# The first loads of a trunk layer split over two queues, and another warm-up of TensorE

## The chip, the cores and the metric

The kernel runs on one core of one Trainium2 chip. The metric is the device time of one execution in microseconds (us), as the median of several runs. Engines are called PE or TensorE (matrix products), DVE or VectorE, ACT or ScalarE, POOL or GpSimd, and SP or SyncE, which only issues transfers here. SPq and ACTq are the queues of transfers that SyncE and ScalarE issue.

## The reference

One layer of a streaming encoder over x of 1024 rows by 1024 features, all in f32:

```python
h = rms_norm(x, mix_norm_g)
proj = h @ w_in                      # columns: u (512), v (512), q (512), k (128), value (128)
y_a = gelu(u) * (W_s layer_norm(gelu(v)) + b)      # W_s: 128 x 128 per group, lower block triangle
y_b = attention over a window of 128 rows, 8 heads, 2 of keys, with sinks and a bias by offset
x = x + concat(rms_norm(y_a), rms_norm(y_b)) @ w_out
h = rms_norm(x, ffn_norm_g)
x = x + (silu(h @ w_gate) * (h @ w_up)) @ w_down   # 2816 features between
return rms_norm(x, final_norm_g)
```

What matters here is the first product only: the v columns of `h @ w_in`. The kernel takes the norm apart. The norm's weight per feature (`mix_norm_g`) is multiplied into the rows of `w_in`, and the root of the mean square per row of x is applied to the result afterwards, so that the products can start on the raw x.

## The kernel before, in words

Each f32 operand is split into a high part, rounded to the type fp32r, and a low part, the rest. A product is then three products in fp32r: high by high, high by low, low by high. ScalarE makes the high part with an activation of the kind Copy (for weights with the norm's weight as scale), VectorE makes the low part by subtracting the high part from the scaled raw data.

The work is written out by hand: every engine has its list of instructions in program order, and semaphores tie them together. No planner is involved. The stage that the change touches is the very first one.

- x arrives transposed, as `xT`, in two halves of 512 rows (h = 0, 1), each in 8 blocks of 128 features (k = 0 to 7). A block is 128 x 512 f32, 256 KB. It goes to `hT_raw[h][:, k]`.
- The v columns of `w_in` arrive in 8 blocks of 128 features by 512 columns, also 256 KB each, in `wv_raw` (line 340). The norm's weights `mix_gT`, 4 KB, go to `mix_g`, a part of the tile `small` (line 339).
- SyncE issues all of this (lines 336 to 340): x block 0, the norm's weights, v block 0, x block 1, v block 1, and so on. The semaphore `block_in[k]` counts 16 for each landed block of k. Behind them it issues the transfers for the attention's bias (`rel_rep`), eight small setup transfers, x's second half and x by rows (`xs`).
- ScalarE (lines 1049 to 1051) takes for each k first x's block (`xT_block`, line 1014), which waits for both blocks of k, then the weights' block (`wv_block`, line 1019). VectorE (lines 1442 to 1444) takes for each k `xT_lo` (line 1391) and then `wv_block` (line 1395).
- PE first runs a warm-up of 20 transposes of the identity (lines 709 to 711), which waits for the identity that POOL makes with a memset and a select (lines 551 to 554). Then come the twelve products of block 0: four of high x by high weights (line 716), four of low x by high weights (line 719), four of high x by low weights (line 722). Blocks 1 to 7 follow through `gate_block`, twelve products each (lines 687 to 689), and block 5 is followed by five transposes of setup data (lines 728 and 730) that need the identity.
- `ones` is a tile of 128 x 128 ones, set by POOL at line 574 and used in the middle of the stage for a sum over rows (line 739). The semaphore `zero_ready` counts this memset and two others.
- The semaphore `block_in[k]` is used again later, for x's second half and for weights of the output projection, with counts that go on from the ones before.

Of the kernel before, what the change touches and what calls it, by code (L numbers as in the profile page):

```python
# [24 lines left out]
def hybrid_trunk_layer(nc, x, xT, mix_gT, w_in, sgu_ln_g, sgu_ln_b, sgu_w, sgu_b, sinks, rel_bias,  # L25
# [3 lines left out]
    P = 128  # L29
    ROWS, D = x.shape  # L30
    T = ROWS // P
    K = D // P
    DA = sgu_ln_g.shape[0]
# [15 lines left out]
    HT = T // 2  # L49
# [4 lines left out]
    def at(name, kb, shape, dtype=F32):  # L54
        n = 4
        for s in shape[1:]:
            n *= s
        offset = BASE + int(kb * 1024)
        assert offset + n <= nc.sbuf_usable_end, name
        return nc.alloc_sbuf_tensor_at(name, shape, dtype, offset=offset)  # L60
# [3 lines left out]
    hT_hi = [at(f"hT_hi{h}", 32 * h, [P, K, C], F32R) for h in range(2)]  # L64
    hT_lo = [at(f"hT_lo{h}", 32 * h + 16, [P, K, C], F32R) for h in range(2)]
    hT_raw = [at(f"hT_raw{h}", 32 * h + 16, [P, K, C]) for h in range(2)]
    wv_hi, wv_lo = at("wv_hi", 64, [P, K, C], F32R), at("wv_lo", 80, [P, K, C], F32R)
# [6 lines left out]
    wv_raw = [at(f"wv_raw{j}", 144 + 4 * j, [P, 2, C]) for j in range(4)]  # L74
# [7 lines left out]
    ident = at("ident", 200.5, [P, P])  # L82
# [3 lines left out]
    vecs, ones = at("vecs", 206, [NV, P]), at("ones", 206.5, [P, P])  # L86
# [64 lines left out]
    def cols(n):  # L151
        c0[0] += n
        assert c0[0] <= 256
        return small[:, c0[0] - n:c0[0]]
# [9 lines left out]
    minus_half, mix_g = cols(T), cols(K)  # L164
# [14 lines left out]
    w_in_k = w_in.rearrange("(k p) n -> p k n", p=P)  # L179
# [60 lines left out]
        return NP * i + IDX[p, m] + 1  # L240


    WARM = 20

    ROOT_BANK, MIX_BANK = (2, 7), (3, 6)

# [2 lines left out]
    with ExitStack() as ctx:  # L249
        ps = ctx.enter_context(nc.psum_tensor("ps", [P, 8, C], F32))  # L250

        def sem(name):
            return ctx.enter_context(nc.semaphore(name))

        ident_set, ident_ready, consts_ready, zero_ready = (sem(n) for n in ("ident_set", "ident_ready", "consts_ready", "zero_ready"))
        mixg_in, rel_in, setup_in, ffng_in, fin_in = (
            sem(n) for n in ("mixg_in", "rel_in", "setup_in", "ffng_in", "fin_in"))
        bias_out, bias_in, rel_built = sem("bias_out"), sem("bias_in"), sem("rel_built")
        setup_T, gains_ready, wT_copied, wT_ready, rowsum_done, Bc_ready, sinks_ready = (
            sem(n) for n in ("setup_T", "gains_ready", "wT_copied", "wT_ready", "rowsum_done", "Bc_ready", "sinks_ready"))  # L260
# [2 lines left out]
        x_sq, x_mse, x_rstd, rstd_T, roots_ready, hT_hi_ready, hT_ready = (  # L263
            sem(n) for n in ("x_sq", "x_mse", "x_rstd", "rstd_T", "roots_ready", "hT_hi_ready", "hT_ready"))

        block_in = [sem(f"block_in{k}") for k in range(K)]
        wv_hi_ready, wv_split = sem("wv_hi_ready"), sem("wv_split")
        va_done, v_ready, v_bn, v_stats, v_mse, v_rstd, vn_ready = (
            sem(n) for n in ("va_done", "v_ready", "v_bn", "v_stats", "v_mse", "v_rstd", "vn_ready"))
# [38 lines left out]
        def _(sp):  # L308
# [5 lines left out]
            def xT_load(h, k):  # L314
                if h:
                    sp.wait_ge(hT_hi_ready, k + 1)
                sp.dma_start(hT_raw[h][:, k, :], xT[h, k]).then_inc(block_in[k], 16)
# [16 lines left out]
                        sp.dma_start(raw[n % 2][:].rearrange("p (k n) -> p k n", k=K), w_in_k[:, :, col:col + P]).then_inc(raw_in[n % 2], 16)  # L334

            for k in range(K):
                xT_load(0, k)
                if k == 0:
                    sp.dma_start(mix_g, mix_gT).then_inc(mixg_in, 16)
                sp.dma_start(wv_raw[k // 2][:, k % 2, :], w_in_k[:, k, DA:2 * DA]).then_inc(block_in[k], 16)  # L340
            sp.dma_start(rel_rep[:].rearrange("p b h -> p (b h)"),
                         rel_bias.rearrange("b h -> (b h)").partition_broadcast(CH)).then_inc(rel_in, 16)
            sp.dma_start(vecs[0:HA, :], group_norm_g[0:DA].rearrange("(k p) -> k p", p=P)).then_inc(setup_in, 16)
# [197 lines left out]
            n = 0  # L541
# [6 lines left out]

        @block.gpsimd
        def _(pool):  # L550
            nc.gpsimd.memset(ident[:], 0.0).then_inc(ident_set, 1)
            nc.gpsimd.memset(minus_half, -0.5).then_inc(consts_ready, 1)
            pool.wait_ge(ident_set, 1)
# [17 lines left out]
                nc.gpsimd.tensor_tensor(rstd_v[:, r:r + 1], ms_v[:, r:r + 1], minus_half[:, 0:1], ALU.pow).then_inc(v_rstd, 1)  # L571

            pool.wait_ge(consts_ready, 1)
            nc.gpsimd.memset(ones[:], 1.0).then_inc(zero_ready, 1)
            nc.gpsimd.memset(kT[:, 0:CH], 0.0).then_inc(zero_ready, 1)
            nc.gpsimd.memset(vT[:, 0:CH], 0.0).then_inc(zero_ready, 1)
            pool.wait_ge(rel_in, 16)
# [105 lines left out]
        def _(pe):  # L683
            mm = nc.tensor.matmul
# [6 lines left out]
            def gate_block(h, k):  # L691
                pe.wait_ge(hT_ready, K * h + k + 1)
                if h == 0:
                    pe.wait_ge(wv_split, k + 1)
                for t in range(HT):
                    rows = slice(t * P, (t + 1) * P)
                    last = split_mm(ps[:, HT * h + t, :], (hT_hi[h][:, k, rows], hT_lo[h][:, k, rows]), (wv_hi[:, k], wv_lo[:, k]), k == 0, k == K - 1)
                    if k == K - 1:
                        last.then_inc(va_done, 1)
# [6 lines left out]
                    last = nc.tensor.transpose(ps[:, ROOT_BANK[h], t * P:(t + 1) * P], rstd_x[:, r:r + 1].to_broadcast([P, P]), ident[:])  # L706
                last.then_inc(rstd_T, 1)

            pe.wait_ge(ident_ready, 1)
            for n in range(WARM):  # L710
                nc.tensor.transpose(ps[:, 0, 0:P], ident[:], ident[:])

            pe.wait_ge(hT_hi_ready, 1)
            pe.wait_ge(wv_hi_ready, 1)
            for t in range(HT):
                mm(ps[:, t, :], hT_hi[0][:, 0, t * P:(t + 1) * P], wv_hi[:, 0], start=True, stop=False)  # L716
            pe.wait_ge(hT_ready, 1)
            for t in range(HT):
                mm(ps[:, t, :], hT_lo[0][:, 0, t * P:(t + 1) * P], wv_hi[:, 0], start=False, stop=False)
            pe.wait_ge(wv_split, 1)  # L720
            for t in range(HT):
                mm(ps[:, t, :], hT_hi[0][:, 0, t * P:(t + 1) * P], wv_lo[:, 0], start=False, stop=False)
            for k in range(1, K):
                gate_block(0, k)
                if k == 5:
                    pe.wait_ge(setup_in, 112)
                    for h in range(HA):
                        last = nc.tensor.transpose(ps[:, 5, h * P:(h + 1) * P], sgu_raw[:, h, :], ident[:])
                    last.then_inc(setup_T, 1)
                    nc.tensor.transpose(ps[:, 4, 0:NV], vecs[:], ident[0:NV, 0:NV]).then_inc(setup_T, 1)  # L730
# [274 lines left out]
        def _(act_e):  # L1005
# [4 lines left out]
                actv(xs[r % 4][:], xs[r % 4][:], ACT.Square, accum_out=ssq_x[:, r:r + 1]).then_inc(x_sq, 1)  # L1010

            def xT_block(h, k):
                act_e.wait_ge(block_in[k], 48 if h else 32)
                actv(hT_hi[h][:, k, :], hT_raw[h][:, k, :], ACT.Copy).then_inc(hT_hi_ready, 1)

            def wv_block(k):
                if k == 0:
                    act_e.wait_ge(mixg_in, 16)
                actv(wv_hi[:, k, :], wv_raw[k // 2][:, k % 2, :], ACT.Copy, scale=mix_g[:, k:k + 1]).then_inc(wv_hi_ready, 1)

            def gated_rows(r):
# [8 lines left out]
            def item(c):  # L1030
# [9 lines left out]
                else:  # L1040
# [5 lines left out]
                        last = actv(w_hi[SLOT[c]][:, k, :], raw[n % 2][:, k * P:(k + 1) * P], ACT.Copy, scale=mix_g[:, k:k + 1])  # L1046
                    last.then_inc(item_hi, 1)

            for k in range(K):
                xT_block(0, k)  # L1050
                wv_block(k)
            for r in range(HT):
                xT_block(1, 2 * r)
                square(r)
                xT_block(1, 2 * r + 1)
# [90 lines left out]
                actv(ps[:, 6, :], ps[:, 6, :], ACT.Square, accum_out=ssqB[:, r:r + 1]).then_inc(yb_squared, 1)  # L1146

            def woB_piece(t):
                act_e.wait_ge(block_in[t], 80)
                if t == 0:  # L1150
                    act_e.wait_ge(unit_done, NU)
                actv(woB_hi[:, t, :], woB_raw[t][:], ACT.Copy, scale=grp_g[:, HA + t:HA + t + 1]).then_inc(woB_hi_ready, 1)
# [53 lines left out]
            for _half in probabilities(1):  # L1206
                pass
            woB_piece(0)
            yb_square(0)
            woB_piece(1)  # L1210
            woB_piece(2)

            for r in range(T):
# [171 lines left out]
        def _(dve):  # L1385
# [3 lines left out]
            def xT_lo(h, k):  # L1389
                dve.wait_ge(hT_hi_ready, K * h + k + 1)  # L1390
                tt(hT_lo[h][:, k, :], hT_raw[h][:, k, :], hT_hi[h][:, k, :].bitcast(F32), ALU.subtract).then_inc(hT_ready, 1)

            def wv_block(k):
                dve.wait_ge(wv_hi_ready, k + 1)
                stt(wv_lo[:, k, :], wv_raw[k // 2][:, k % 2, :], mix_g[:, k:k + 1], wv_hi[:, k, :].bitcast(F32), ALU.mult, ALU.subtract).then_inc(wv_split, 1)
# [44 lines left out]
                last.then_inc(sinks_ready, 1)  # L1440

            for k in range(K):
                xT_lo(0, k)
                wv_block(k)
            xT_lo(1, 0)
            setup_copies()
            for k in range(1, K):
# [414 lines left out]
```

## Time and profile before

| | us |
|---|---|
| median of 3 runs | 939.16 |
| lowest and highest | 938.81, 939.39 |
| the profiled execution | 939.3 |
| its span, first to last instruction | 937.5 |
| PE busy | 927.8 |
| DVE busy | 550.2 |
| ACT busy | 409.1 |
| POOL busy | 318.1 |

The span is what the profiler sees between the first and the last instruction; the profiled execution's own time is a little longer, since it holds what lies around the span. Busy time counts an engine's instructions, the warm-up's too. For an idle time the profile names what ended it, the releaser. A matmul's listed duration includes its way through the array, so that the products of a row overlap: their pace is read from the starts.

### The profile page before, as it was taken

What the parts mean: (1) busy time and instruction counts of PE and PEld (TensorE: products, weight loads), DVE (VectorE), ACT (ScalarE), POOL (GpSimd) and SP (SyncE); (2) the same over time, 40 slices, a digit from 0 to 9 for tenths busy, and PEclk for the clock granted to TensorE, in tenths of its full rate; (3) what the DMA queues carried; (4) which work ended last, traced back from release to release, by engine and by line L of the source; (5) the groups of instructions that cost most, each with busy time, mean ns of one, the idle gap of its engine ahead of it and who ended that gap; (6) DMA issues with size and microseconds to landing.
All of it is one profiled execution on the core that took longest, in us unless ns stands there. A gap on an engine that the chain in (4) does not pass through costs nothing.

```text
span 937.5 us, 12052 instructions
## 1 busy us (share of the span) xinstructions
PE 927.8 (99%) x4327; PEld 763.8 (81%) x4327; DVE 550.2 (59%) x798; ACT 409.1 (44%) x896; POOL 318.1 (34%) x330
## 2 busy tenths in 40 slices
PE   9999999999999999999999999999999999999997
PEld 7888888878788788888888888888888888888885
DVE  5754653476676995574645546546455766545653
ACT  6843560456554733333333333333245354444351
POOL 1410000000005396585674955747554100000022
PEclk9999999999999999999999999999999999999999
DMA  9621231411214425537346274373648996665643
GB/s 328 225 78 64 71 80 64 90 46 66 93 48 154 124 77 193 162 107 237 112 157 220 65 233 142 116 224 100 193 159 279 334 389 194 193 199 186 199 134 136
DMA packets 131999, 147.03 MB, mean 157 GB/s; under 512 B 16280, under 2 KB 92644, under 8 KB 131940
## 3 DMA queue, kind: packets, MB, share of 16 engines
q1 hardware_dynamic: 131412, 145.87, 47.9%
q8 instruction: 35, 0.57, 0.2%
q10 hardware_dynamic: 528, 0.39, 0.1%
q14 instruction: 24, 0.20, 0.1%
HBM read 105.73 MB, written 40.50 MB: 156 GB/s over the span
## 4 chain that ended last, share of the span: by engine, by line
PE 97%; DVE 1%; issue 0%; DMA 0%; ACT 0%; SPq 0%; DVEq 0%; POOLq 0%; POOL 0%; ACTq 0%
PE ps L687 31%; PE ps L689 31%; PE ps L688 31%; PE ps L889 1%; PE ps L816 1%; PE ps L762 1%; PE ps L835 1%; PE ps L826 1%; DVE woB_lo L1578 0%; PE ps L842 0%; PE ps L770 0%; DMA wv_raw<-in_w_in 0%; PE ps L780 0%; PE ps L716 0%; DVE small L1556 0%
## 5 line engine op out<-in xcount | busy, mean ns | idle before, releaser
L1654 DVE TENSOR_TENSOR P_lo<-P_raw,P_hi 128x512 fp32r<-128x512 f32 x132 | 120.6, 929 | 79.8 <-ACT P_hi L1199 78.6
L687 PE MATMUL ps<-T_hi,P_hi 128*128 128x512 f32 x352 | 137.0, 389 | 0.4 <-issue 0.4
L689 PE MATMUL ps<-T_hi,P_lo 128*128 128x512 f32 x352 | 136.9, 389 | 0.0
L688 PE MATMUL ps<-T_lo,P_hi 128*128 128x512 f32 x352 | 136.9, 389 | 0.0
L687 PE MATMUL ps<-rb_hi,ra_hi 128*128 128x512 f32 x308 | 119.8, 389 | 0.0
L688 PE MATMUL ps<-rb_lo,ra_hi 128*128 128x512 f32 x308 | 119.8, 389 | 0.0
L689 PE MATMUL ps<-rb_hi,ra_lo 128*128 128x512 f32 x308 | 119.8, 389 | 0.0
L635 POOL TENSOR_TENSOR wd<-wd 128x256 f32<-128x256 f32 x88 | 79.7, 905 | 96.3 <-DMA wd<-in_w_down 91.1
L1297 ACT ACTIVATE ra_hi<-ra 128x512 fp32r<-128x512 f32 x77 | 48.6, 631 | 99.2 <-DMA rb<-w_down_T 62.0
L558 POOL TENSOR_SCALAR small<-small 128x1 f32<-128x1 f32 (+2 forms) x11 | 2.2, 197 | 225.0 <-ACT ps L1146 131.2
L687 PEld LDWEIGHTS ps<-T_hi,P_hi 128*128 128x128 f32 x352 | 66.1, 188 | 14.5 <-issue 0.8
L1199 ACT ACTIVATE P_hi<-P_raw 128x512 fp32r<-128x512 f32 x132 | 76.6, 620 | 2.1 <-POOL P_raw L606 2.1
L688 PEld LDWEIGHTS ps<-T_lo,P_hi 128*128 128x128 f32 x352 | 66.1, 188 | 13.7
L689 PEld LDWEIGHTS ps<-T_hi,P_lo 128*128 128x128 f32 x352 | 66.1, 188 | 13.6
L1732 DVE TENSOR_TENSOR ra_lo<-ra,ra_hi 128x512 fp32r<-128x512 f32 x77 | 55.4, 720 | 36.7 <-ACT ra_hi L1297 36.3
L687 PE MATMUL ps<-B,P_hi 128*128 128x512 f32 x176 | 68.8, 391 | 0.4 <-DVE P_lo L1654 0.4
L558 POOL TENSOR_SCALAR late<-late 128x1 f32<-128x1 f32 x12 | 5.8, 484 | 184.8 <-ACT junk L1365 178.9
L688 PE MATMUL ps<-B,P_hi 128*128 128x512 f32 x176 | 68.5, 389 | 0.0
L689 PE MATMUL ps<-B,P_lo 128*128 128x512 f32 x176 | 68.5, 389 | 0.0
L689 PEld LDWEIGHTS ps<-rb_hi,ra_lo 128*128 128x128 f32 x308 | 57.8, 188 | 12.1
L687 PEld LDWEIGHTS ps<-rb_hi,ra_hi 128*128 128x128 f32 x308 | 57.8, 188 | 12.0
L688 PEld LDWEIGHTS ps<-rb_lo,ra_hi 128*128 128x128 f32 x308 | 57.8, 188 | 11.9
(200 smaller groups left out, 1944.8 us busy)
## 6 DMA issues: line engine op xcount, KB each, us to landing
wd<-in_w_down SPq DMA_DIRECT2D x44, 256.0 KB, 3.4
w_down_T<-wd SPq DMA_DIRECT2D x22, 512.0 KB, 5.1
ra<-act_S SPq DMA_DIRECT2D x44, 256.0 KB, 2.7
rb<-w_down_T SPq DMA_DIRECT2D x44, 256.0 KB, 3.0
act_S<-Q SPq DMA_DIRECT2D x33, 256.0 KB, 3.7
ra<-act_A SPq DMA_DIRECT2D x33, 256.0 KB, 4.7
rb<-in_w_down SPq DMA_DIRECT2D x33, 256.0 KB, 5.6
P_raw<-in_w_gate SPq DMA_DIRECT2D x22, 256.0 KB, 3.9
```

Of the source, the lines that this page charges most:

```text
L635: nc.gpsimd.tensor_tensor(wd[:, d, :], wd[:, x, :], wd[:, y, :], ALU.subtract).then_inc(wd_summed, 1)
L687: mm(dst, lhs[0], rhs[0], start=start, stop=False, skip_group_check=onto)
L688: mm(dst, lhs[0], rhs[1], start=False, stop=False, skip_group_check=onto)
L689: return mm(dst, lhs[1], rhs[0], start=False, stop=stop, skip_group_check=onto)
L762: last = mm(ps[:, MIX_BANK[m % 2], t * P:(t + 1) * P], vn[:, HT * half + t, h * P:(h + 1) * P], sgu_wT[:, h, :], start=True, stop=True)
L816: last = mm(ps[:, 3 + g, (2 * ci + tp) * P:(2 * ci + tp + 1) * P], q, kT[rows, c * CH:c * CH + WIN], start=True, stop=True)
L826: last = nc.tensor.transpose(ps[:, 5, (2 * g + tp) * P:(2 * g + tp + 1) * P], S[:, g, ci, tp, :], ident[:])
L835: last = mm(ps[g * DH:(g + 1) * DH, 6, ci * G * CH:(ci + 1) * G * CH], V2[:, 2 * r + ci, g, :], pT[:, ci, g * G * CH:(g + 1) * G * CH], st ...
L1199: actv(w_h[p, m][:], src[:], ACT.Copy).then_inc(w_hi_ready, 1)
L1297: actv(ra_hi[n][:], ra[n][:], ACT.Copy).then_inc(step_hi, 1)
L1654: tt(w_l[p, m][:], src[:], w_h[p, m][:].bitcast(F32), ALU.subtract).then_inc(w_split, 1)
L1732: tt(ra_lo[n][:], ra[n][:], ra_hi[n][:].bitcast(F32), ALU.subtract)
```

## The change

- v's blocks 0, 1 and 2 and the norm's weights are issued by ScalarE, ahead of its first activation: block 0, the norm's weights, block 1, block 2. A new semaphore `wv0_in`, in the place of `mixg_in`, counts v's block 0 and the norm's weights. SyncE issues x's blocks 0 to 2 one after the other, and from k = 3 on v's block ahead of x's.
- ScalarE and VectorE take the weights' block ahead of x's for each k. In block 0, PE takes high x by low weights second and low x by high weights last.
- The warm-up is 10 products of `ones` with 64 columns of `ones`, into another bank (7), and waits for the memset of `ones`, which POOL now does first of all. The wait for the identity moves to block 5.
- Because `block_in[0]` now counts only x's block, the later waits on these semaphores go by the list `LOADED`.

```diff
-    WARM = 20
+    WARM, WARM_N = 10, 64
...
+        LOADED = [16 if k == 0 else 32 for k in range(K)]
...
             for k in range(K):
+                if k >= 3:
+                    sp.dma_start(wv_raw[k // 2][:, k % 2, :], w_in_k[:, k, DA:2 * DA]).then_inc(block_in[k], 16)
                 xT_load(0, k)
-                if k == 0:
-                    sp.dma_start(mix_g, mix_gT).then_inc(mixg_in, 16)
-                sp.dma_start(wv_raw[k // 2][:, k % 2, :], w_in_k[:, k, DA:2 * DA]).then_inc(block_in[k], 16)
...
         def _(pool):
+            nc.gpsimd.memset(ones[:], 1.0).then_inc(zero_ready, 1)
             nc.gpsimd.memset(ident[:], 0.0).then_inc(ident_set, 1)
...
             pool.wait_ge(consts_ready, 1)
-            nc.gpsimd.memset(ones[:], 1.0).then_inc(zero_ready, 1)
...
-            pe.wait_ge(ident_ready, 1)
+            pe.wait_ge(zero_ready, 1)
             for n in range(WARM):
-                nc.tensor.transpose(ps[:, 0, 0:P], ident[:], ident[:])
+                mm(ps[:, 7, 0:WARM_N], ones[:], ones[:, 0:WARM_N], start=True, stop=True)
...
                 mm(ps[:, t, :], hT_hi[0][:, 0, t * P:(t + 1) * P], wv_hi[:, 0], start=True, stop=False)
+            pe.wait_ge(wv_split, 1)
+            for t in range(HT):
+                mm(ps[:, t, :], hT_hi[0][:, 0, t * P:(t + 1) * P], wv_lo[:, 0], start=False, stop=False)
             pe.wait_ge(hT_ready, 1)
             for t in range(HT):
                 mm(ps[:, t, :], hT_lo[0][:, 0, t * P:(t + 1) * P], wv_hi[:, 0], start=False, stop=False)
-            pe.wait_ge(wv_split, 1)
-            for t in range(HT):
-                mm(ps[:, t, :], hT_hi[0][:, 0, t * P:(t + 1) * P], wv_lo[:, 0], start=False, stop=False)
             for k in range(1, K):
                 gate_block(0, k)
                 if k == 5:
+                    pe.wait_ge(ident_ready, 1)
...
             def xT_block(h, k):
-                act_e.wait_ge(block_in[k], 48 if h else 32)
+                act_e.wait_ge(block_in[k], LOADED[k] + 16 * h)
...
                 if k == 0:
-                    act_e.wait_ge(mixg_in, 16)
+                    act_e.wait_ge(wv0_in, 32)
+                else:
+                    act_e.wait_ge(block_in[k], LOADED[k])
...
+            act_e.dma_start(wv_raw[0][:, 0, :], w_in_k[:, 0, DA:2 * DA]).then_inc(wv0_in, 16)
+            act_e.dma_start(mix_g, mix_gT).then_inc(wv0_in, 16)
+            for k in (1, 2):
+                act_e.dma_start(wv_raw[k // 2][:, k % 2, :], w_in_k[:, k, DA:2 * DA]).then_inc(block_in[k], 16)
             for k in range(K):
+                wv_block(k)
                 xT_block(0, k)
-                wv_block(k)
...
             for k in range(K):
+                wv_block(k)
                 xT_lo(0, k)
-                wv_block(k)
```

## Rows read from the trace of the kernel before

**Rows 1.** The page: busy time by engine, and the chain that ended last by engine

```profile
PE 927.8 (99%) x4327; PEld 763.8 (81%) x4327; DVE 550.2 (59%) x798; ACT 409.1 (44%) x896; POOL 318.1 (34%) x330
...
PE 97%; DVE 1%; issue 0%; DMA 0%; ACT 0%; SPq 0%; DVEq 0%; POOLq 0%; POOL 0%; ACTq 0%
```

**Rows 2.** Waits of PE, whole span: waiter, releaser, us in total, times, longest

```profile
PE ps L711 <- POOL ident L554: 1.5, 1, 1.5
PE ps L687 <- issue: 0.7, 2, 0.4
```

**Rows 3.** The chain of waits, 0 to 10 us: start, us, what

```profile
1.64 3.22 DMA wv_raw<-in_w_in
...
4.88 0.63 ACT hT_hi L1014
5.51 0.62 ACT wv_hi L1019
...
6.27 1.68 PE ps L716 x4
```

**Rows 4.** Timeline, 0 to 10 us: start, us, engine, line, operation, tiles

```profile
0.72 0.20 POOL L551 MEMSET ident<- 128x128 f32 x1 [0.29 <-POOLq L1846]
0.72 0.39 SPq L317 DMA_DIRECT2D hT_raw<-in_xT  x1
0.73 1.28 ACT L1014 ACT_TABLE_LOAD   x1 [0.73 <-PEq L1846]
...
1.17 0.42 SPq L339 DMA_DIRECT2D small<-in_mix_gT  x1
...
1.51 4.53 PE L711 MATMUL ps<-ident 128*128 128x128 f32 x20 [1.51 <-POOL ident L554]
...
6.54 0.63 ACT L1014 ACTIVATE hT_hi<-hT_raw 128x512 fp32r<-128x512 f32 x1 [0.41 <-DMA wv_raw<-in_w_in]
...
7.78 1.09 PE L719 MATMUL ps<-wv_hi,hT_lo 128*128 128x512 f32 x4
...
7.82 0.75 DVE L1395 SCALAR_TENSOR_TENSOR wv_lo<-wv_raw,small,wv_hi 128x512 fp32r<-128x512 f32 x1
...
8.71 1.08 PE L722 MATMUL ps<-wv_lo,hT_hi 128*128 128x512 f32 x4
...
9.63 0.39 PE L687 MATMUL ps<-wv_hi,hT_hi 128*128 128x512 f32 x1
```

**Rows 5.** DMA issues at 0.72, 1.17, 1.64, 2.58 us: KB, us to landing

```profile
hT_raw<-in_xT SPq DMA_DIRECT2D x1, 256.0 KB, 2.6
...
small<-in_mix_gT SPq DMA_DIRECT2D x1, 4.0 KB, 2.3
...
wv_raw<-in_w_in SPq DMA_DIRECT2D x1, 256.0 KB, 3.2
...
wv_raw<-in_w_in SPq DMA_DIRECT2D x1, 256.0 KB, 3.9
```

**Rows 6.** Windows: us, busy by engine, granted PE clock, DMA share, GB/s

```profile
1.50:4.25 2.75, 2.73 (x13) 2.74 (x14) 0.00 (x0) 0.51 (x1) 0.29 (x3) 1.00 0.88 197
4.50:6.50 2.00, 1.77 (x9) 1.40 (x8) 0.95 (x2) 1.24 (x2) 0.00 (x0) 1.00 1.02 377
```

**Rows 7.** Timeline of ScalarE, 31 to 33 and 43 to 45 us

```profile
31.32 1.28 ACT L1026 ACT_TABLE_LOAD   x1 [0.97 <-POOL small L560]
...
43.96 0.61 ACTq L1065 DMA_DIRECT2D bias_by_offset<-by_offset  x1
```

**Rows 8.** Single lines 711, 728, 716: duration ns min/median/max, first and last start

```profile
L711 PE MATMUL ps<-ident x20: 421/421/476, 1.5 to 5.6; 128*128 128x128 f32 x20
...
L728 PE MATMUL ps<-ident,sgu_raw x4: 272/272/273, 23.2 to 23.6; 128*128 128x128 f32 x4
...
L716 PE MATMUL ps<-wv_hi,hT_hi x4: 397/542/767, 6.3 to 7.5; 128*128 128x512 f32 x4
L719 PE MATMUL ps<-wv_hi,hT_lo x4: 387/395/397, 7.8 to 8.5; 128*128 128x512 f32 x4
```

**Rows 9.** Line 739 (one f32 product in the code), and the chain at 158 us

```profile
L739 PE MATMUL ps<-sgu_wT,ones x2: 590/590/591, 43.2 to 43.6; 128*128 128x512 f32 x2
...
158.64 1.09 PE ps L816 x16
```

More of the change, by code:

```diff
@@ L255, in hybrid_trunk_layer @@
         ident_set, ident_ready, consts_ready, zero_ready = (sem(n) for n in ("ident_set", "ident_ready", "consts_ready", "zero_ready"))
-        mixg_in, rel_in, setup_in, ffng_in, fin_in = (
-            sem(n) for n in ("mixg_in", "rel_in", "setup_in", "ffng_in", "fin_in"))
+        wv0_in, rel_in, setup_in, ffng_in, fin_in = (
+            sem(n) for n in ("wv0_in", "rel_in", "setup_in", "ffng_in", "fin_in"))
         bias_out, bias_in, rel_built = sem("bias_out"), sem("bias_in"), sem("rel_built")
@@ L1148, in woB_piece @@
             def woB_piece(t):
-                act_e.wait_ge(block_in[t], 80)
+                act_e.wait_ge(block_in[t], LOADED[t] + 48)
                 if t == 0:
```

## The prediction

> **What bounds the kernel now.** The page's busy table comes first: PE is busy 927.8 of a span of 937.5 us and holds 97% of the chain that ended last [rows 1]. So a change can only pay where PE stands still or runs slowly: 9.7 us in all. The waits of PE say where: 1.5 us before its first instruction, and little after that [rows 2]. The beginning of the chain of waits shows what the busy table hides: from 1.51 to 6.04 us PE is busy with transposes that compute nothing, and the useful work begins at 6.27 us. What ends last before that is a transfer: the block of v's weights, issued at 1.64 us, landed 3.22 us later, at 4.86; then ScalarE copies x's block and the weights' (4.88 and 5.51), and the first product follows at 6.27 [rows 3]. From there the products run on without a gap that the waits show, to the end phase. The forecast is therefore about one number: how much earlier the second block of products (k = 1), which starts at 9.63 us now [rows 4], starts afterwards. Everything behind it is PE-bound and moves with it.
>
> **Part 1, the order of the first transfers.** Now SyncE's queue issues x's block 0 at 0.72, the norm's weights at 1.17 and v's block 0 at 1.64. They land after 2.6, 2.3 and 3.2 us, at 3.3, 3.5 and 4.86 [rows 3, 4, 5]. After the change x's block and v's block 0 are both issued at about 0.72, on two queues, and the norm's weights behind v's block at about 1.2. The issue alone gains 0.92 us for v's block, but the bytes are the same. In the stretch 1.50 to 4.25 the chip moved 197 GB/s, that is 542 KB, which is the two blocks of 256 KB and the small transfer; from 4.50 on it moved 377 GB/s [rows 6]. Ends of the estimate for the moment A at which all three have landed:
> - if the early rate belongs to the one queue, two queues reach the later rate: 524 KB at 377 GB/s is 1.4 us; x's block of 256 KB by itself landed at 3.3 and took 262/197 = 1.3 us of that, so both would land near 3.4, and the norm's weights a little later;
> - if the early rate belongs to the time since the start, both blocks are complete no earlier than now, 4.86, and the norm's weights, now last and sharing with x's block 1, may come 0.3 us later: 5.2.
>
> ScalarE has a floor of its own. It issues four transfers first. SyncE's cost 0.47 us each from start to start (0.72, 1.17, 1.64) [rows 3, 4]; the only one that ScalarE issues now takes 0.61 [rows 7]. So they end at 0.72 + 4 x 0.47 = 2.6 to 0.72 + 4 x 0.65 = 3.3. Then comes its table load of 1.28 us, which now starts at 0.73 and is hidden [rows 4]. The second table load of this trace stands directly ahead of the activation that needs it [rows 7], so I put the first one behind the four issues: ScalarE is free at 3.9 to 4.6. It stays hidden if A is later. If it stood ahead of them instead, v's block would be issued at 2.0 and land at 2.0 + 3.2 = 5.2, the same upper end.
> I take A = 4.3, between 3.9 and 5.2 and a little nearer to the early end, because the small transfer no longer separates the two blocks. The order of the two copies on ScalarE (weights first) leaves their sum alone: PE wants both, and 6.27 - 4.88 = 1.39 us from A to the first product stays [rows 3]. The first product starts at 4.3 + 1.4 = 5.7 in place of 6.27: **0.55 us gained** (ends: 0.98 and -0.3).
>
> The Trainium skill speaks against this part: "DMA: Bandwidth & Descriptors", section "Issuing engines are not separate DMA queues", says that transfers started by several engines share the same 16 DMA engines, and that more issuers save only the issue time. By it the sum of this part would be near zero and rival 2 would hold.
>
> **Part 2, the order inside block 0.** PE's second four products now take the weights' low half, and the high times low half of x comes last. VectorE makes the weights' low half first (0.75 us, started when ScalarE's first copy is done), then x's. The first is ready about 0.2 us after PE's first product starts and is wanted 0.93 us after it (the spacing of four products: 7.78, 8.71, 9.63 [rows 4]); the second is ready about 0.9 us after, wanted 1.86 after. Cost: nothing, as now; without this cover the later one would cost its 0.69 us.
> Is block 1 in time? Now ScalarE begins with it at 6.54 and VectorE ends at 7.82 + 0.75 = 8.57, that is 2.03 us later, and PE starts it at 9.63: 1.06 us to spare [rows 4]. Its weights landed at 2.6 + 3.9 = 6.5 [rows 5]. Afterwards four blocks precede or include it on the two queues as now, so by the rates of rows 6 it lands at about 6.1: ready 8.1 to 8.2. That caps the whole gain at 9.63 - 8.15 = 1.5 us. Later blocks need 512 KB per 2.78 us and get 377 GB/s, so they are covered twice over.
>
> **Part 3, the warm-up and PE's clock.** The granted clock in the windows reads 1.00 (2.4 GHz) throughout, from 1.50 us on [rows 6]. The durations say otherwise: each of the 20 transposes took 421 ns and they follow each other at 4.53/20 = 0.226 us, where the same form takes 272 ns later [rows 4, 8]. The first four products start over 7.78 - 6.27 = 1.51 us, where the next fours take 0.93 [rows 4]; their durations run up to 767 ns, against at most 397 for the next four [rows 8]. So PE ran at the lower level (1.2 GHz) up to roughly 7.5 us, and **0.58 us** of useful work was lost, some three products at 0.2 us each.
> The change replaces 20 transposes from 1.51 by 10 products of ones from about 0.95 (0.20 us of memset behind POOL's start at 0.72, with the 0.03 us of hand-over as now). An f32 product is two matmul instructions in this trace [rows 9], so it is again 20. Bounds of one: 0.226 us if it costs what a transpose did, half of that, 0.113, if the time goes with the 64 columns instead of 128 (16 others with 64 rows took 1.09/16 = 0.07 at the higher level [rows 9], so the weight load does not forbid it). The warm-up ends between 0.95 + 2.3 = 3.2 and 0.95 + 4.5 = 5.5, before 5.7 in each case: no delay of PE itself, but possibly up to 2.5 us of idle time ahead of the first useful product. What the clock does with it no row shows. Ends: no slow product left (+0.58), or all twelve of block 0 slow, 12 x 0.2 = 2.4 in place of 0.58 (-1.8). PE starts 0.56 us sooner and does real products, the first useful one starts 0.55 us sooner too. I take half of the present loss: **0.3 us gained**.
>
> The skill's "TensorE: Matmul & The Clock Gate", section "Part 4: PE-mode transpose", says that transposes do not count as activity for the higher clock as products do. The trace does not contradict it: 4.5 us of transposes saw no fast one, and the clock rose some 1.2 us into the products. By it the products of ones would bring the higher level before 5.7 and the whole 0.58 would come back; that is rival 1.
>
> **Part 4, what costs nothing.** POOL's first memset delays the identity by 0.2 us; it is now first wanted after block 5, where the transposes start at 23.2 us today [rows 8], so the wait added there is met. SyncE issues four transfers fewer, so the small setup transfers and x's rows are issued up to 1.9 us earlier, into a stretch in which the transfers' rate is the limit; their bytes are unchanged. PE waits for none of them now [rows 2].
>
> **The sum.** 0.55 + 0.3 = 0.85 us off a span of 937.5. The profiled execution took 939.3 us and the median of the runs is 939.16, so the span leaves 1.8 us outside, which the change does not touch: 938.45 for a profiled run, 938.3 for the median.
>
> **Rivals.**
> 1. Both halves at their best: two queues carry the first blocks at the later rate, A is set by ScalarE's table load at 3.9 (gain 0.98), and the clock is high from the first product (0.58). Sum 1.56, capped at 1.5: 937.7. For it: the dip between the first transfers. Against it: the rate was low for 2.75 us, across three transfers.
> 2. The transfers share what there is: A stays at 4.8 to 5.2, because the norm's weights now land last. Gain of the start 0 to -0.3, clock +0.3: 939.2. For it: the 197 GB/s of rows 6. Against it: v's block was the last of one queue, and the dip is not needed.
> 3. Slower: the warm-up takes 2.3 us and leaves a pause of some 2.5 us, and the clock stays low through block 0 and beyond. Twelve slow products cost 2.4 us in place of 0.58, minus 0.55 for the start: +1.3, so 940.4. It decides from the sixth slow product on, since (0.55 + 0.58)/0.2 is 5.7. For it: 4.5 us of back to back instructions did not raise the clock now, and fewer will come. Against it: they start earlier and are of another kind.
>
> **How the numbers follow.** Forecast (937.9 to 938.9) 0.48; rival 1 0.17; rival 2 0.20; rival 3 0.15. The runs before spread over 0.6 us, so each case has 0.3 us of scatter. The range runs from 937.3 (rival 1 with scatter) to 939.9 (rival 2 with scatter and the mild part of rival 3). A measurement of this kernel can tell about 0.2%, 1.9 us, from no change. Faster than 937.3 needs more than the cap of 1.5 us: 0.07. Slower than 941.0 needs the lower clock for nearly twenty products: 0.04. Within: 0.89.
>
> **What would show it.** Of the profile after: v's block 0 issued by ScalarE's queue at about 0.7 and the first activation at 4.3 (below 4.0: rival 1; above 4.7: rival 2); the table load behind the four issues; the twelve products of block 0 in 2.8 to 3.1 us from start to start; block 1 at about 8.8 in place of 9.63; matmul durations in the warm-up, and a long idle time of PE between it and block 0 if rival 3 is at work. I am wrong if block 1 starts later than 9.6, or if a new wait of PE appears in the first blocks.

## The result: slower, by two microseconds at the start

The median of 18 runs of the changed kernel is 941.40 us (940.54 to 941.89), that of 18 runs of the kernel before 939.32. The ratio is 1.0018, with a 95% interval of 1.0012 to 1.0025. The forecast was 938.3, with a range from 937.3 to 939.9.

The chain of waits of the changed kernel, 0 to 12 us (start, us, what), answers to rows 3:

```profile
0.73 0.41 ACTq L1053
1.17 4.11 DMA small<-in_mix_gT
5.31 0.72 ACT wv_hi L1023
6.03 0.53 ACT hT_hi L1016
6.60 2.08 PE ps L717 x4
8.68 1.71 PE ps L720 x4
10.38 1.46 PE ps L723 x4
```

The reader is to see two things. The transfer that ends last is no longer a block of 256 KB but the 4 KB of the norm's weights: issued at 1.17, landed 4.11 us later, at 5.28. And the three lots of four products that follow take 2.08, 1.71 and 1.46 us. The timeline of the same stretch answers to rows 4:

```profile
0.98 4.53 PE L712 MATMUL ps<-ones 128*128 128x64 f32 x20 [0.98 <-POOL ones L552]
...
2.62 1.28 ACT L1023 ACT_TABLE_LOAD   x1 [2.62 <-issue]
...
6.60 2.08 PE L717 MATMUL ps<-wv_hi,hT_hi 128*128 128x512 f32 x4 [1.10 <-ACT hT_hi L1016]
...
8.47 1.91 PE L720 MATMUL ps<-wv_lo,hT_hi 128*128 128x512 f32 x4
...
10.18 1.66 PE L723 MATMUL ps<-wv_hi,hT_lo 128*128 128x512 f32 x4
...
11.68 0.40 PE L688 MATMUL ps<-wv_hi,hT_hi 128*128 128x512 f32 x1
```

The useful work starts at 6.60 us (6.27 before) and block 1 at 11.68 (9.63 before, [rows 4]). The twelve products of block 0 take 11.68 - 6.60 = 5.08 us from start to start in place of 3.36. The durations of single products in lines 717, 720 and 723 (ns, min/median/max) answer to rows 8, where 387 to 397 ns was the pace of the higher clock:

```profile
L717 PE MATMUL ps<-wv_hi,hT_hi x4: 632/632/796, 6.6 to 8.0; 128*128 128x512 f32 x4
...
L720 PE MATMUL ps<-wv_lo,hT_hi x4: 632/632/632, 8.5 to 9.8; 128*128 128x512 f32 x4
...
L723 PE MATMUL ps<-wv_hi,hT_lo x4: 394/604/632, 10.2 to 11.4; 128*128 128x512 f32 x4
```

Ten of the twelve took the full 632 ns or more, the eleventh 577, the last 394: the lower level (1.2 GHz) held until the eleventh. As before, the granted clock in the windows does not show it; columns are us, busy of PE, PEld, DVE, ACT and POOL, granted clock, DMA share, GB/s:

```profile
1.50:4.25 2.75, 2.75 (x15) 2.75 (x14) 0.00 (x0) 1.28 (x1) 0.29 (x3) 1.00 0.87 278
...
6.60:11.68 5.08, 5.08 (x12) 4.03 (x13) 4.67 (x8) 4.50 (x8) 0.00 (x0) 1.00 1.05 396
```

The first of these two also answers to rows 6: two queues moved 278 GB/s in the stretch in which one moved 197, and still the first product came later. The DMA issues at 0.72, 0.73 and 1.17 us show why (KB, us to landing): x's block 0 landed at 4.3, v's block 0 at 4.5, the small transfer behind it at 5.28.

```profile
hT_raw<-in_xT SPq DMA_DIRECT2D x1, 256.0 KB, 3.6
wv_raw<-in_w_in ACTq DMA_DIRECT2D x1, 256.0 KB, 3.8
...
small<-in_mix_gT ACTq DMA_DIRECT2D x1, 4.0 KB, 4.1
```

PE's waits, against rows 2: two at the start, and the same small ones behind. The wait ahead of block 0 was 0.23 us before and is 1.10 now.

```profile
PE ps L717 <- ACT hT_hi L1016: 1.1, 1, 1.1
PE ps L712 <- POOL ones L552: 1.0, 1, 1.0
PE ps L688 <- issue: 0.7, 2, 0.4
```

**The books close.** The profiled run took 941.35 us and started block 1 at 11.68: the rest is 929.67. Before it was 939.3 - 9.63 = 929.67. In all seventeen profiled kernels of this study that rest lies between 929.61 and 929.84. So the start of block 1 carries the whole difference, as the prediction had it, and it splits in two: +0.33 us in the start of the first product, +1.72 us in the duration of block 0.

### The profile page after: what moved, and what is told of

Read it like the earlier page. It is cut to its first block, busy times and chain, and to the rows that moved or that the text cites. A ratio compares the mean times of both kernels' runs of the same rounds, so it can differ in the third digit from the quotient of the medians.

```text
span 939.5 us, 12053 instructions
## 1 busy us (share of the span) xinstructions
PE 929.5 (99%) x4327; PEld 765.5 (81%) x4327; DVE 550.6 (59%) x798; ACT 409.1 (44%) x896; POOL 315.4 (34%) x330
## 4 chain that ended last, share of the span: by engine, by line
PE 97%; DVE 1%; DMA 0%; issue 0%; ACT 0%; DVEq 0%; POOLq 0%; ACTq 0%; POOL 0%
PE ps L688 31%; PE ps L690 30%; PE ps L689 30%; PE ps L891 1%; PE ps L818 1%; PE ps L764 1%; PE ps L837 1%; PE ps L828 1%; DVE woB_lo L1586 0%; DMA small<-in_mix_gT 0%; PE ps L844 0%; PE ps L772 0%; PE ps L717 0%; PE ps L782 0%; PE ps L720 0%
```

## The experiments

Times are medians of 11 runs (5 where it is said); the kernel before, run beside each group, had 939.24 to 939.33. "First product", "block 0" (its duration, from start to start) and "block 1" are from each one's profiled run, in us; E11's block 0 holds a wait of 1.02 us.

| kernel | first product | block 0 | block 1 | profiled run | median |
|---|---|---|---|---|---|
| before | 6.27 | 3.36 | 9.63 | 939.30 | 939.32 |
| changed | 6.60 | 5.08 | 11.68 | 941.35 | 941.40 |
| E1 before, 64-column warm-up | 6.92 | 4.75 | 11.67 | 941.34 | 941.34 |
| E2 changed, transposes | 6.74 | 2.90 | 9.64 | 939.32 | 939.33 |
| E3 changed, 128 columns | 6.67 | 2.85 | 9.52 | 939.14 | 939.30 |
| E4 changed, norm's weights first | 6.57 | 5.29 | 11.86 | 941.70 | 941.05 |
| E5 before, no warm-up | 7.56 | 4.70 | 12.26 | 941.93 | 941.33 |
| E6 changed, 12 products of 64 | 6.61 | 4.91 | 11.52 | 941.16 | 941.27 |
| E7 changed, 5 of 512 columns | 6.74 | 2.98 | 9.72 | 939.35 | 939.50 |
| E8 E3, norm's weights by POOL | 9.15 | 5.04 | 14.19 | 943.81 | 943.73 |
| E9 before, 4 of 512 columns | 6.75 | 3.17 | 9.92 | 939.61 | 939.57 |
| E10 E3, x first | 6.42 | 4.66 | 11.08 | 940.74 | 939.18 |
| E11 E3, norm's weights first on SyncE | 5.51 | 4.03 | 9.54 | 939.28 | 939.27 |
| E12 x first, 4 of 512 columns | 6.76 | 3.14 | 9.90 | 939.60 | 939.53 |
| E13 E11, two blocks on ScalarE | 5.52 | 2.92 | 8.44 | 938.05 | 938.41 |
| E14 E13's loads, 3 of 512 | 5.47 | 3.17 | 8.64 | 938.30 | 938.46 |
| E15 E13's loads, 64 columns | 5.68 | 4.23 | 9.91 | 939.63 | 939.99 |

### The warm-up: E1, E2, E3, E5, E6, E7

**E1**, the kernel before with the new warm-up alone:

```diff
-    WARM = 20
+    WARM, WARM_N = 10, 64
...
-                nc.tensor.transpose(ps[:, 0, 0:P], ident[:], ident[:])
+                mm(ps[:, 7, 0:WARM_N], ones[:], ones[:, 0:WARM_N], start=True, stop=True)
```

> The kernel before with the new warm-up alone: 10 products of ones with 64 columns, started after POOL's first memset. Theory W (the warm-up's 64-column products do not bring the higher clock, transposes of 128 columns do): the first product stays at 6.27 us, all twelve products of block 0 are slow, block 1 starts at about 11.3 and the time is 939.3 + 1.7 = 941.0. Theory P (only the pause between warm-up and block 0 counts, 1.1 us in the changed kernel): the pause is 6.27 - 5.51 = 0.76 us, so a part of the loss, 939.3 to 941.0. Theory L (the loads' new order alone costs, the warm-up is harmless): 939.3.

941.34 us (ratio 1.0021, 1.0012 to 1.0030). By the medians the warm-up alone makes the whole loss. The profiled run splits it otherwise than the changed kernel's: v's block 0 landed at 5.51 us in it, 0.65 later than in the profile of before, so of its 2.04 us 0.65 are a later first product and 1.39 a slower block 0.

**E2**, the changed kernel with the old warm-up (the same lines in the other direction, and POOL's memsets in the old order):

> The changed kernel with the old warm-up of 20 transposes (1.51 to 6.04 us), all else as changed. Theory W: the clock is high after three or four products of block 0 again; only the later first product remains (6.60 against 6.27, +0.33): 939.6. Theory P: the pause is 0.56 us, between the 0.23 of before and the 1.1 of the changed kernel: 939.6 to 940.8. Theory L: 941.4 as the changed kernel.

939.33 us (1.0002, 0.9993 to 1.0011): the loss is gone, with all the new loads in place. The clock rose within these transposes: the ones started up to 4.8 us took 421 ns or more, the last ones 272, the pace of the higher level in rows 8.

```profile
L712 PE MATMUL ps<-ident x5: 272/273/421, 4.8 to 5.4; 128*128 128x128 f32 x5
```

**E3**, one number in the changed kernel:

```diff
-    WARM, WARM_N = 10, 64
+    WARM, WARM_N = 10, 128
```

> The changed kernel with 128 columns in place of 64 in each of the 10 warm-up products. The warm-up should last as long as now (20 instructions at 0.226 us, 0.98 to 5.51) and leave the same pause of 1.1 us. Theory W: the clock rises as early as with transposes or earlier: 939.0 to 939.6. Theory P: the pause is unchanged and so is the time: 941.4. Theory L: 941.4.

939.30 us (1.0005, 0.9996 to 1.0014). Its warm-up and its first four products, beside the changed kernel's above:

```profile
0.98 4.64 PE L712 MATMUL ps<-ones 128*128 128x128 f32 x20 [0.98 <-POOL ones L552]
```

```profile
6.67 1.20 PE L717 MATMUL ps<-wv_hi,hT_hi 128*128 128x512 f32 x4 [1.06 <-ACT hT_hi L1016]
```

The warm-up starts at the same moment, lasts as long to 0.1 us, and leaves the same pause (1.06 us against 1.10). Twice the columns in the same instructions, and the four products take 1.20 in place of 2.08 us. So it is neither the pause nor the length of the warm-up nor products against transposes: it is how wide the warm-up's products are.

**E5**, the kernel before with `WARM = 0`:

> The kernel before without any warm-up. It prices the warm-up as a whole. Theory W in its strict form (10 products of 64 columns are worth nothing to the clock): the same time as the kernel before with the 64-column warm-up, 941.3. Theory W in a weak form (they are worth something, but less than transposes): slower than that, 941.6 to 942.5. If the clock simply rises a fixed time after the first instruction of PE: the rise comes at 6.27 + 6 = 12.3 us in place of 7.5, which costs more again, 941.8 and up.

941.33 us (1.0018, 1.0009 to 1.0027), within 0.1 us of the two kernels with 64-column products. In this kernel those products bought nothing measurable. Here too the profiled run holds a late landing (v's block 0 at 6.16 us), so that 1.29 of its 2.63 us are a later first product.

**E6**, `WARM, WARM_N = 12, 64`, which closes the pause:

> The changed kernel with 12 products of 64 columns in place of 10: the warm-up lasts to 0.98 + 24 x 0.226 = 6.4 us and leaves 0.2 us before the first product instead of 1.1. Theory W: no better, 941.2 to 941.5. Theory P (the pause counts once the warm-up is of the thin kind): 939.4 to 940.5.

941.27 us. PE waits only 0.24 us ahead of block 0 and the products are slow all the same:

```profile
0.98 5.38 PE L712 MATMUL ps<-ones 128*128 128x64 f32 x24 [0.98 <-POOL ones L552]
```

```profile
6.61 2.07 PE L717 MATMUL ps<-wv_hi,hT_hi 128*128 128x512 f32 x4 [0.24 <-ACT hT_hi L1016]
```

**E7**, products of 512 columns (`ones` read four times):

```diff
-                mm(ps[:, 7, 0:WARM_N], ones[:], ones[:, 0:WARM_N], start=True, stop=True)
+                mm(ps[:, 7, :].rearrange("p (a n) -> p a n", n=P), ones[:], ones[:].unsqueeze(1).to_broadcast([P, 4, P]), start=True, stop=True)
```

> The changed kernel with 5 products of ones of 512 columns (10 instructions of about 0.43 us each at the lower clock, 0.98 to about 5.3). Theory W: at least as good as 128 columns, 939.3 or, if wider ones bring the clock up before block 0, down to 938.9. If 128 columns already give all there is: 939.3. Theory P: the pause is 1.2 us or more, 939.3 and up.

939.50 us (1.0002, 0.9994 to 1.0011). The warm-up was to last to 5.3 us and lasted to 6.7: an instruction was put at 0.43 us, and at the lower clock they follow each other at some 0.86. Within the warm-up one sees the clock rise: the first rows of line 712 are those of products started up to 3.7 us, the last those from 4.8 us on (ns, min/median/max).

```profile
L712 PE MATMUL ps<-ones x3: 867/1061/1061, 2.0 to 3.7; 128*128 128x512 f32 x3
```

```profile
L712 PE MATMUL ps<-ones x3: 593/593/593, 4.8 to 5.7; 128*128 128x512 f32 x3
```

The same form takes 590 ns in the middle of the kernel [rows 9]. The one started at 3.7 us took 867 ns, so the higher clock came while it ran; block 0 ran at it from its first product.

### The loads: E4, E8, E10, E11

**E4**, the small transfer ahead of v's block 0 on ScalarE's queue:

```diff
-            act_e.dma_start(wv_raw[0][:, 0, :], w_in_k[:, 0, DA:2 * DA]).then_inc(wv0_in, 16)
             act_e.dma_start(mix_g, mix_gT).then_inc(wv0_in, 16)
+            act_e.dma_start(wv_raw[0][:, 0, :], w_in_k[:, 0, DA:2 * DA]).then_inc(wv0_in, 16)
```

> The changed kernel with the norm's weights (4 KB) ahead of v's block 0 on ScalarE's queue. All theories agree on the start: the 4 KB land at 3.0 to 3.5 instead of 5.28, v's block 0 at 4.5 to 4.9 instead of 4.5, so the first product starts at 5.9 to 6.3 instead of 6.60. Theory W: block 0 stays slow throughout and the gain of the start shows in full, 0.3 to 0.7: 940.7 to 941.1. Theory P: the pause falls from 1.1 to 0.4 to 0.8 us, and the clock comes back as well: 939.5 to 940.5.

941.05 us. The time lies where theory W had it (0.35 us below the changed kernel's, too little to tell from no gain), and block 0 stayed slow as it said (5.29). The start, on which all theories agreed, is a miss: the first product came at 6.57. The small transfer landed at 0.73 + 3.1 = 3.8, and v's block 0 at 1.17 + 4.1 = 5.3. In both orders what stands second on ScalarE's queue landed at 5.3.

**E8**, E3 with the small transfer issued by POOL, behind its first memset (5 runs; ScalarE's first activation then waits for two semaphores):

> The changed kernel with 128 columns in the warm-up and the norm's weights issued by POOL, on a third queue, behind its first memset. If the 4 KB behind v's block 0 are what now ends last (5.28 us, where v's block 0 landed at 4.5 and x's at 4.3), the first product starts at 4.5 + 1.35 = 5.9 instead of 6.67, and with the clock as in the run with 128 columns the time is 938.5 to 939.0. If the clock rises at a fixed moment (about 7.2 us), half of the 0.75 us is given back: 938.9. If the transfers only trade places (the landing moves to another of the three), 939.3.

943.73 us (1.0044, 1.0032 to 1.0057), the worst of all. Its chain of waits:

```profile
1.28 5.22 DMA small<-in_mix_gT
...
6.52 0.02 ACTq L1022
...
6.57 1.28 ACT L1025
7.86 0.72 ACT wv_hi L1025
8.58 0.53 ACT hT_hi L1017
...
9.15 2.08 PE ps L718 x4
```

Three things went wrong together. POOL's transfer took 5.22 us. ScalarE's table load, which in the changed kernel ran at 2.62 us before any data were there, started only behind it: one of the two waits stands as an instruction of its own ahead of the load (ACTq L1022, a semaphore instruction of 0.02 us), so 1.28 us that were hidden became visible. And PE stood still for 3.5 us; block 0 then took 5.04 us although the warm-up was the good one. That this pause cost the clock is likely, but no run varied it alone.

**E10**, E3 with x's block copied first, which does not need the norm's weights (and the same exchange in VectorE's list):

```diff
             for k in range(K):
-                wv_block(k)
                 xT_block(0, k)
+                wv_block(k)
```

> The changed kernel with 128-column warm-up products, and ScalarE and VectorE taking x's block ahead of the weights' in each k, as before the change. Theory G (the 4 KB of the norm's weights, landing at 5.3, are what ends last, and the weights-first order puts both copies behind them): x's copy starts at 4.3 to 4.5, the weights' at 5.3, the first product at 6.1 instead of 6.67: 0.5 us less than with the same warm-up and weights first (939.3), 938.8. Rival (the order of the two copies is neutral, as the prediction had it): 939.3.

939.18 us (0.9999, 0.9990 to 1.0008) against E3's 939.30 and 938.8 expected: inconclusive in time. The mechanism shows in the trace of ScalarE: x's copy runs while the small transfer is still under way, and the first product comes 0.89 us after that landing (5.53 to 6.42) where it is 1.32 in E3 (5.35 to 6.67).

```profile
4.52 0.63 ACT L1016 ACTIVATE hT_hi<-hT_raw 128x512 fp32r<-128x512 f32 x1 [0.61 <-DMA hT_raw<-in_xT]
5.55 0.72 ACT L1023 ACTIVATE wv_hi<-wv_raw,small 128x512 fp32r<-128x512 f32 x1 [0.41 <-DMA small<-in_mix_gT]
```

Its profiled run is one in which the clock rose late in spite of the 128-column warm-up (block 0: 4.66 us, 940.74 us). Times of that size come with transposes and 128 columns in some runs: above 940.4 us were 2 of 11 in E2, 3 in E3, 2 in E10, none in E11, 3 of the 18 of the kernel before and 7 of its 120 beside the experiments. With 64 columns or none they are the rule (18 of 18 of the changed kernel, 10 of 11 in E1 and in E5).

**E11**, E3 with the small transfer first on SyncE's queue:

> The changed kernel with 128-column warm-up products, and the norm's weights issued first of all on SyncE's queue, ahead of x's block 0. Theory G: they land at about 3.1; x's block 0, issued at 1.2, and v's block 0 land at 4.3 to 4.8, so the first product starts at 5.7 to 6.2 and the time is 938.5 to 938.9. Rival (putting the 4 KB ahead of a block only delays that block, as on ScalarE's queue, where v's block 0 then landed at 5.25): 939.3.

939.27 us, where the rival had it, but not for the rival's reason: x's block 0 did land later (4.8 against 4.3), and the first product started at 5.51 all the same. And then:

```profile
PE ps L689 <- DVE hT_lo L1399: 1.0, 1, 1.0
```

```profile
1.64 5.71 DMA hT_raw<-in_xT
7.38 0.73 ACT wv_hi L1024
8.13 0.75 DVE wv_lo L1403
8.89 0.61 DVE hT_lo L1399
9.54 0.50 PE ps L689
```

Block 1 of x landed at 7.35, and from there it takes 2.2 us over ScalarE and VectorE to the products. A new wait of 1.02 us took the place of the one removed.

### The wide warm-up with other loads: E9, E12

**E9** is the kernel before, **E12** the changed kernel with x first, both with 4 products of 512 columns.

> The kernel before with the warm-up alone exchanged for 4 products of ones with 512 columns (8 instructions, 0.98 to about 6.0 us, of which the later ones should already run at the higher clock, as in the run with 5 of them). Theory W: the clock is high from block 0's first product, block 0 takes 2.8 us; with the loads as before (first product at 6.27 in one profile, 6.92 and 7.56 in two others with the same loads) block 1 starts 0 to 0.6 us sooner than with transposes: 938.7 to 939.3. If the loads' moment decides instead of the clock: 939.3.

> The changed kernel with x's copy first, as in the run before this but one, and 4 warm-up products of 512 columns. Theories W and G together: first product at 6.1 at the higher clock, block 1 at 8.9 instead of 9.6: 938.6. If the warm-up ends after 6.1 it delays block 0 by what it is longer.

939.57 and 939.53 us: both misses, by 0.3 and 0.9 of the main forecasts. Their warm-ups lasted to about 6.75 us, longer than computed, because the clock rose late within them (at some 6 us, in both), and held up data that in E9 was ready at 4.90 + 1.39 = 6.3 (its first copy on ScalarE began at 4.90). E12's second sentence had named this case. No run of the four kernels with 512 columns was above 940.3 us.

### Putting it together: E13, E14, E15

**E13** is E11 with v's block 2 back on SyncE's queue, so that it is issued behind x's block 1 (at 2.11 us) and not beside it. Its edit against the changed kernel, apart from `WARM_N = 128`:

```diff
+            sp.dma_start(mix_g, mix_gT).then_inc(wv0_in, 16)
             for k in range(K):
-                if k >= 3:
+                if k >= 2:
...
-            act_e.dma_start(mix_g, mix_gT).then_inc(wv0_in, 16)
-            for k in (1, 2):
-                act_e.dma_start(wv_raw[k // 2][:, k % 2, :], w_in_k[:, k, DA:2 * DA]).then_inc(block_in[k], 16)
+            act_e.dma_start(wv_raw[0][:, 1, :], w_in_k[:, 1, DA:2 * DA]).then_inc(block_in[1], 16)
```

> The changed kernel with the norm's weights first on SyncE's queue, only v's blocks 0 and 1 on ScalarE's, and 128-column warm-up products. Theory B (block 1's landing is the second bound, 7.35 us in the run with three blocks on ScalarE's queue): four blocks and 4 KB precede nothing else, so block 1 lands at 5.8 to 6.3, its halves are ready at 7.9 to 8.3, and block 1's products follow block 0's (5.5 + 2.8 = 8.3) without a wait: 1.2 us less than now, 938.0 to 938.3. Rival (the bound is elsewhere, the loads' order is worth nothing): 939.2.

938.41 us, 0.84 below the kernel before beside it (0.9989, 0.9980 to 0.9998, an interval that ends just below 1), against 938.0 to 938.3 expected. This is the version that beats both.

```profile
0.97 4.63 PE L713 MATMUL ps<-ones 128*128 128x128 f32 x20 [0.97 <-POOL ones L553]
...
5.52 1.24 PE L718 MATMUL ps<-wv_hi,hT_hi 128*128 128x512 f32 x4
...
6.60 1.08 PE L721 MATMUL ps<-wv_lo,hT_hi 128*128 128x512 f32 x4
...
7.52 1.08 PE L724 MATMUL ps<-wv_hi,hT_lo 128*128 128x512 f32 x4
...
8.44 0.39 PE L689 MATMUL ps<-wv_hi,hT_hi 128*128 128x512 f32 x1
```

No wait stands between the warm-up and block 0, nor between block 0 and block 1, and ScalarE began with block 1 at 5.63 us instead of 7.38 in E11. Now the warm-up's end at 5.5 is itself what block 0 waits for: the data were ready a moment earlier.

**E14** has the same loads and 3 products of 512 columns:

> The same loads with 3 products of 512 columns as warm-up (6 instructions of 0.43 to 0.85 us: it ends between 4.5 and 6.1). Theory B with the clock high from block 0 on: 938.0 to 938.3, and 938.6 where the warm-up lasts beyond 5.5.

938.46 us (0.9992, 0.9983 to 1.0001), the same as E13, and 0.2 above the 938.0 to 938.3 expected.

**E15** has the same loads and the 64-column warm-up:

> The same loads with the 64-column warm-up of the changed kernel. Theory W (its products are worth nothing to the clock, whatever the loads do): all twelve products of block 0 slow, 5.5 + 5.1 = 10.6, some 1 us less than the changed kernel's 11.6: 940.2 to 940.5. If the clock rises at a fixed moment near 11.5 us instead: block 1 is slow too and the time stays at 940.9.

939.99 us (1.0006, 0.9997 to 1.0015). Six or seven of the twelve products were slow in the profiled run, not twelve; its runs spread from 939.00 to 940.86. The expected 10.6 for block 1 was missed (9.91). So the clock's cost is not a constant of the warm-up: the loads' gain remains beside it and the moment of the rise varies. On these loads 128 columns in place of 64 are worth 1.6 us.

This profile also limits what E13's shows. The loads are the same, and yet x's block 1 landed at 7.6 us here (6.2 in E14, 5.6 in E13), later than in E11:

```profile
7.66 0.72 ACT L1024 ACTIVATE wv_hi<-wv_raw,small 128x512 fp32r<-128x512 f32 x1 [2.02 <-DMA hT_raw<-in_xT]
```

So the gain of E13 and E14 over E11 stands in the medians (938.41 and 938.46 against 939.27), but that it comes by an earlier landing of block 1 rests on single profiles that scatter by 2 us, and is not shown.

## Why the prediction was wrong

**Right.** PE from block 1 on was the bound, and the whole change is the shift of block 1's start; the rest was 929.67 us before and after. The table load went behind the four issues and stayed hidden (2.62 to 3.90). The warm-up again took 20 instructions and 4.53 us, the upper of the two bounds. The order within block 0 brought no wait of PE, and the moved wait for the identity cost nothing.

**Wrong, the step that turned the sign: part 3.** It read that the lower clock cost 0.58 us, took half of it as a gain because PE "starts 0.56 us sooner and does real products", and so forecast +0.3 where block 0 lost 1.72 (5.08 against 3.36). The bound "all twelve of block 0 slow" was the outcome: it was priced at 2.4 us, and 5.08 - 2.78 = 2.30 came, in place of 0.58. What failed is the reading of the transposes: because none of the 20 ran fast, they were taken for poor at raising the clock. E5 shows what they were worth: without them the same kernel takes 2.1 us more. The right question was what block 0 would cost without the warm-up, and no row of before answers it. The edit halved the columns of the warm-up's instructions, and E3 shows that this one number is the loss.

The Trainium skill's sentence about transposes ("TensorE: Matmul & The Clock Gate", "Part 4: PE-mode transpose") was weighed as agreeing with the trace. The runs say the opposite here: 20 transposes of 128 columns gave 939.33 (E2), no warm-up 941.33 (E5), 10 products of 64 columns 941.40, and products of 128 columns, 939.30 (E3), did no better than transposes.

**Rival 3** named the place, and 1.3 us of loss for the 2.05 measured, but not the cause. It put it on the pause; with 0.24 us of pause (E6) the loss stays, and with 1.06 us (E3) it is gone.

**Mis-sized: part 1.** A was put at 4.3 and came at 5.28, outside the range given up to 5.2, so the first product was late by 0.33 instead of early by 0.55. Both large blocks landed as forecast, at 4.3 and 4.5. The small transfer did not: it was given "a little later" in the early end and "0.3 us later" in the late one, and took 0.8 behind v's block. That the order of the two copies on ScalarE "leaves their sum alone" holds only when all that they need lands together; here weights first put x's copy behind the small transfer as well, 0.4 us (E10's 0.89 against E3's 1.32). The 0.33 itself is measured against one profile in which v's block 0 landed early (4.86; 5.51 in E1 and 6.16 in E5 with the same loads). E2, with the new loads and the old warm-up, has the median of before (939.33), so over the runs the new loads with that warm-up neither gained nor lost.

**Mis-sized: the cap.** Block 1 was to land at 6.1 and be ready at 8.15. In the changed kernel v's block 1 landed at 6.95; PE did not wait for it, since block 0 took so long. In E11, with three of v's blocks on the second queue, x's block 1 landed at 7.35 and the products could start at 9.54; with two (E13) they followed without a wait. The Trainium skill's rule in "DMA: Bandwidth & Descriptors", "Issuing engines are not separate DMA queues", by which a second issuer saves only its issue time, made rival 2 here. The runs do not contradict it: the queues gained nothing in E2 and E3, and the 0.84 us of E13 are no more than the 0.91 by which v's block 0 is issued earlier (0.73 in place of 1.64).

**The chances.** Slower than 941.0 was given 0.04. It was said to need the lower clock for nearly twenty products, and that is wrong by the prediction's own ends: a start later by 0.3 and twelve slow products (1.8) add up to 2.1 us, 941.3. The two bad ends were never added, and that sum is what came (0.33 and 1.72). With no row on which kind of work brings the clock, the case deserved much more than 0.04.

## What to carry to other kernels

A warm-up of TensorE is judged by what follows it, not by the speed of its own instructions: run the kernel once without it, and treat the width of its instructions as part of what it does. Where a first product waits for several transfers, the smallest one counts like the others: look where it lands, try it ahead of the large ones on either queue (on ScalarE's it only moved the late landing to v's block, E4; first on SyncE's the first product came at 5.51, E11), and do first the work that does not need it. When a start is moved earlier, compute the next block's landing with all that shares the queues, since the wait removed tends to come back one block later.

## What the runs showed of the hardware that was not expected

- With instructions of 64 columns for 4.5 us PE's clock stayed at its lower level as it does without any (941.34 and 941.33); with 128 columns over the same 4.5 us it was, by their times, high in most runs for block 0. Read from the durations, the rise came at 4 to 7.5 us in nine profiles with transposes, 128 or 512 columns, at about 10 in E10 and 13.5 in E8; with 64 columns or none it came at 11 to 12 in five profiles and at about 9 in E15.
- A transfer of 4 KB behind one of 256 KB on ScalarE's queue landed 0.8 us after it, while two other blocks were under way; through POOL's queue it took 5.22 us (E8), through SyncE's 2.3 to 2.6.
- With one queue in the order of before, v's block 0, issued at 1.64, landed at 4.9 in two profiles (before, E9) and at 5.51 and 6.16 in two others (E1, E5); with the two queues of the change the last of the three landings lay within 5.2 to 5.6 in eight profiles. What makes the scatter stays open.
- Also open: why the clock rises late in some runs with the same program (E3: 3 of 11), why it rose at about 9 us in E15 and at 11 in E6 with nearly the same pause behind the same kind of warm-up, and whether a pause of 3.5 us by itself brings it down (E8).
